# A MoE pair loop: the scatter chunks as one block behind the up product, and the gate multiply ahead of the adds

## The chip, the cores and the metric

The kernel runs on one core of a Trainium2 chip, as one launch. The metric is the device time of that launch in microseconds; lower is better.

## What is computed

The program is one inference step of a small hybrid decoder: 256 prompt tokens and 32 sample tokens (288 in all), width 1024, two layers. Each layer has a token mixer (recurrence and window attention in the first, dilated attention in the second), a normalisation, and a mixture of 64 experts. Only the expert part bears on the change:

```python
gate = jnp.take_along_axis(scores, top_e, axis=1)
gate = gate / jnp.sum(gate, -1, keepdims=True) * ROUTED_SCALE
...
def expert_block(args):
    xb, e = args
    hb = jax.nn.silu(xb @ w_gate[e]) * (xb @ w_up[e])
    return hb @ w_down[e]
...
routed = jax.ops.segment_sum(y_sorted.astype(F32) * gate_sorted[:, None], tok_sorted, num_segments=N)
```

For each expert the tokens routed to it are picked out, put through a SwiGLU of width 256, multiplied by their gates, and added back to the rows of the tokens.

## The kernel before

Experts are taken two at a time. Such a pair is numbered n, and q = n % 2 says which half of the double buffers it uses. Each layer has 32 pairs. Every engine runs its own program, and semaphores alone tie them together; the order on an engine is the order in which the code is written. TensorE (PE) does, for pair n, in `step`:

- `gather_pe` (L1200): the tokens of the pair, 64 slots for each of the two experts, are picked out of the bf16 parts of the activations by a matrix of zeros and ones that GpSimd made. It comes in two halves of 28 matmuls.
- `hidden_pe` (L1236): two transposes of the hidden values of pair n-1. It waits for `s_h2`, which VectorE signals when it has multiplied by the gate.
- `turn_pe` (L1208, L1211): the pick matrix is turned for the way back.
- `down_pe` (L1247): the down product of pair n-1, in fp32.
- `up_pe` (L1225): the gate and up products of pair n, in fp32. Eight slices `c` of the width, two experts each; the outputs of the two experts lie in partitions 0 to 63 and 64 to 127 of the same bank. An fp32 matmul shows as two MATMUL records, so a slice `c` is four records, and the whole product 32. Behind the last slice PE signals `s_gu`.
- `scatter_pe` (L1260): the outputs of pair n-1 are spread back over the 288 token rows. Eight chunks of 128 features; each is three bf16 matmuls of 288 columns (three parts of the fp32 value) into bank 6 or 7, by turns.

ScalarE (ACT) takes the silu (L1345) when `s_gu` comes. VectorE (DVE) then multiplies silu, up product and the gate of the slot (L1388, `hidden`), and adds each scattered chunk to the accumulator in SBUF (L1395, `add`). DVE also forms the second and third bf16 part of the down product (L1377, L1382, `outputs`).

Two waits matter for the change. A scatter chunk writes the bank of the chunk two before it, so it waits until that one has been added:

```python
pe.wait_ge(s_add[L], NC * n + c + NC - 1)
```

and an add waits for its chunk (`s_scat`). The sync queue (SP) fetches the experts' weights. The gate and up weights of a pair two ahead are issued (L1772) when `s_gu` says that the slots have been read, the down weights (L1779) on `s_dn`, which `down_pe` signals.

`over_pairs` runs `first` for pair 0, `step` for pairs 1 to 31, and `last` for what is left of pair 31. In `last` the eight scatter chunks stand one behind another with nothing between them.

Of the kernel before, what the change touches and what calls it, by code (L numbers as in the profile page):

```python
# [27 lines left out]
NC = D // P  # L28
# [100 lines left out]
def build(nc, a, o):  # L129

    ctx = ExitStack()
    with ctx:
# [86 lines left out]
        def slot_of(m):  # L219
            return m % RING  # L220
# [972 lines left out]
        def gather_pe(pe, L, n, q, hf):  # L1193

            pe.wait_ge(s_pm[L], 7 * n + 13)
            for c in range(4 * hf, 4 * hf + 4):
                for k in range(7):
                    m = 3 * NSA if k == 6 else P
                    lhs = xb[0:m, k].rearrange("t (f c) -> t c f", c=NC)[:, c, :]
                    ins = pe.matmul(ps[:, hf, (c % 4) * P:(c % 4 + 1) * P], lhs, pm[0:m, q, k // 3, :],  # L1200
                                    start=k == 0, stop=k == 6)
            ins.then_inc(s_ga[L], 1)

        def turn_pe(pe, L, n, q):

            for t in range(3):
                m = ROWS[t]
                pe.transpose(ps[:, 3, :].bitcast(BF16)[:, t * P:t * P + m], pm[0:m, q, t, :], ident_b[0:m, 0:m])  # L1208
            for t in range(3):
                m = ROWS[t]  # L1210
                ins = pe.matmul(ps[:, 3, NT:NT + 1], MO["pg"][0:m, q, t, :], ones[0:m, 0:1], start=t == 0, stop=t == 2)  # L1211
            ins.then_inc(s_pgt[L], 1)

        def up_pe(pe, L, n, q, it, scatter=None):

            pe.wait_ge(s_xg[L], 2 * n + 2)
            for u in range(2):
                s = slot_of(EXP0[L] + 2 * q + u)  # L1220
                pe.wait_ge(s_ring[L][s], static_dma[L][s] + (it + 1) * 32)
            for c in range(NC):
                for u in range(2):
                    w = ring[:, slot_of(EXP0[L] + 2 * q + u), 0:4096].rearrange("p (g c n) -> p c g n", g=2, c=NC)
                    ins = pe.matmul(ps[64 * u:64 * u + CAP, 2, :], MO["xg"][:, c, u * CAP:(u + 1) * CAP], w[:, c],  # L1225
                                    start=c == 0, stop=c == NC - 1)
                if c == NC - 1:
                    ins.then_inc(s_gu[L], 1)
                for chunk in {4: (0, 1), 5: (2, 3), 6: (4, 5), 7: (6, 7)}.get(c, ()) if scatter else ():
                    scatter(chunk)  # L1230

        def hidden_pe(pe, L, n):

            pe.wait_ge(s_h2[L], n + 1)
            for j in range(2):
                ins = pe.transpose(ps[:, 2, j * P:(j + 1) * P], MO["h"][:, j * P:(j + 1) * P], ident)  # L1236
            ins.then_inc(s_ht[L], 1)

        def down_pe(pe, L, n, q, it):

            pe.wait_ge(s_htc[L], n + 1)
            pe.wait_ge(s_ring_dn[L][q], (it + 1) * 32)
            for hf in range(2):
                for j in range(2):
                    for u in range(2):
                        w = ring[:, slot_of(EXP0[L] + 2 * q + u), 4096:6144].rearrange("p (j n) -> p j n", j=2)
                        ins = pe.matmul(ps[64 * u:64 * u + CAP, 4 + hf, :], MO["hT"][:, j, 64 * u:64 * u + CAP],  # L1247
                                        w[:, j, hf * BANK:(hf + 1) * BANK], start=j == 0, stop=j == 1)
            ins.then_inc(s_dn[L], 1)

        def scatter_pe(pe, L, n, q, c):

            if c == 0:
                pe.wait_ge(s_yc[L], 4 * n + 4)
                pe.wait_ge(s_pgtc[L], n + 1)

            pe.wait_ge(s_add[L], NC * n + c + NC - 1)
            for k in range(3):
                lhs = yb[:, k].rearrange("p (f c) -> p c f", c=NC)[:, c, :]
                ins = pe.matmul(ps[:, 6 + c % 2, 0:NT], lhs, pgt[:, q, :], start=k == 0, stop=k == 2)  # L1260
            ins.then_inc(s_scat[L], 1)

        def over_pairs(eng, L, first, step, last):

            more = iterations(eng)
            first(0, 0, 0)
            with eng.Fori(0, more) as i:
                step(2 * i + 1, 1, i)
                step(2 * i + 2, 0, i + 1)
            step(2 * more + 1, 1, more)  # L1270
            last(2 * more + 1, 1, more)
            return more

        def moe_pairs_pe(pe, L):
            pe.wait_ge(s_acc0, 8 * L + NC)
            pe.wait_ge(s_disp, L + 1)
            pe.wait_ge(s_xb, 10 * (L + 1))

            def first(n, q, it):
                gather_pe(pe, L, n, q, 0)  # L1280
                gather_pe(pe, L, n, q, 1)
                turn_pe(pe, L, n, q)
                up_pe(pe, L, n, q, it)

            def step(n, q, it):
                gather_pe(pe, L, n, q, 0)
                hidden_pe(pe, L, n - 1)
                gather_pe(pe, L, n, q, 1)
                turn_pe(pe, L, n, q)

                down_pe(pe, L, n - 1, 1 - q, it if q else it - 1)
                up_pe(pe, L, n, q, it, lambda c: scatter_pe(pe, L, n - 1, 1 - q, c))

            def last(n, q, it):
                hidden_pe(pe, L, n)
                down_pe(pe, L, n, q, it)
                for c in range(NC):
                    scatter_pe(pe, L, n, q, c)

            more = over_pairs(pe, L, first, step, last)  # L1300

            pe.wait_ge(s_add[L], more * (2 * NC) + 3 * NC)
            for t in range(3):
                m = ROWS[t]
                for c in range(NC):
                    ins = pe.transpose(ps[0:m, 2 * t + c // 4, (c % 4) * P:(c % 4 + 1) * P],
                                       MO["acc"][:, c, t * P:t * P + m], ident)
                ins.then_inc(s_f, 1)
# [58 lines left out]
        def moe_pairs_dve(v, L):  # L1367
            v.wait_ge(s_disp, L + 1)
            v.wait_ge(s_acc0, 8 * L + NC)
            v.sem_inc(s_add[L], NC)  # L1370

            def outputs(n):

                for hf in range(2):
                    half = slice(hf * BANK, (hf + 1) * BANK)
                    v.wait_ge(s_yb[L], 4 * n + hf + 1)
                    v.tensor_tensor(MO["y_rest"][:, half], ps[:, 4 + hf, :], yb[:, 0, half],  # L1377
                                    ALU.subtract).then_inc(s_yc[L], 1)
                for hf in range(2):
                    half = slice(hf * BANK, (hf + 1) * BANK)  # L1380
                    v.wait_ge(s_yb[L], 4 * n + hf + 3)
                    v.tensor_tensor(yb[:, 2, half], MO["y_rest"][:, half], yb[:, 1, half],  # L1382
                                    ALU.subtract).then_inc(s_yc[L], 1)

            def hidden(n, q):

                v.wait_ge(s_si[L], n + 1)
                v.scalar_tensor_tensor(out=MO["h"], in0=MO["sg"], scalar=MO["own_gate"][:, q:q + 1],  # L1388
                                       in1=ps[:, 2, DE:2 * DE], op0=ALU.mult, op1=ALU.mult).then_inc(s_h2[L], 1)

            def add(n, chunks=range(NC)):
                for c in chunks:
                    v.wait_ge(s_scat[L], NC * n + c + 1)
                    v.wait_ge(s_add[L], NC * n + c + 1)
                    v.tensor_tensor(MO["acc"][:, c, :], MO["acc"][:, c, :], ps[:, 6 + c % 2, 0:NT],  # L1395
                                    ALU.add).then_inc(s_add[L], 1)

            def first(n, q, it):
                hidden(n, q)

            def step(n, q, it):
                outputs(n - 1)
                add(n - 1, range(NC - 2))
                hidden(n, q)
                add(n - 1, range(NC - 2, NC))

            def last(n, q, it):
                outputs(n)
                add(n)

            more = over_pairs(v, L, first, step, last)
            v.wait_ge(s_add[L], more * (2 * NC) + 3 * NC)

# [717 lines left out]
```

## Time and profile before

| | |
|---|---|
| time, median of 3 runs | 1954.39 us (1952.23 to 1955.93) |
| span of the profiled execution | 1949.9 us |
| PE busy | 1825.8 us, 94% |
| DVE busy | 634.4 us, 33% |
| ACT busy | 471.5 us, 24% |
| GpSimd busy | 531.6 us, 27% |
| HBM | 305 GB/s over the span |

The profile gives the span from the first to the last instruction; of the profiled execution no other time is shown, and the median of the runs is 4.5 us above its span. PE stands for matmuls and PEld for the loading of their stationary operand, which goes on beside them.

### The profile page before, as it was taken

What the parts mean: (1) busy time and instruction counts of PE and PEld (TensorE: products, weight loads), DVE (VectorE), ACT (ScalarE), POOL (GpSimd) and SP (SyncE); (2) the same over time, 40 slices, a digit from 0 to 9 for tenths busy, and PEclk for the clock granted to TensorE, in tenths of its full rate; (3) what the DMA queues carried; (4) which work ended last, traced back from release to release, by engine and by line L of the source; (5) the groups of instructions that cost most, each with busy time, mean ns of one, the idle gap of its engine ahead of it and who ended that gap; (6) DMA issues with size and microseconds to landing.
All of it is one profiled execution on the core that took longest, in us unless ns stands there. A gap on an engine that the chain in (4) does not pass through costs nothing. (4 is left out here: it accounts for less than half of the span.)

```text
span 1949.9 us, 31977 instructions
## 1 busy us (share of the span) xinstructions
PE 1825.8 (94%) x11784; PEld 1119.5 (57%) x11784; DVE 634.4 (33%) x1444; ACT 471.5 (24%) x968; POOL 531.6 (27%) x1045
## 2 busy tenths in 40 slices
PE   7789999999999999978998978799999999999994
PEld 5563755555555555546777865375555555555552
DVE  4431523333232323342002343332323333333325
ACT  1431422222222222221002222322222222222222
POOL 1000453434333343201200000154343434243411
PEclk9859799999999999998997579889999999999997
DMA  9997188878888787845695355628787878787860
GB/s 309 334 321 255 65 324 319 345 310 337 320 325 331 316 343 309 347 160 218 212 331 205 129 184 184 274 89 333 314 343 308 345 312 347 310 343 314 341 263 25
DMA packets 113860, 540.81 MB, mean 277 GB/s; under 512 B 18821, under 2 KB 22661, under 8 KB 79636
## 3 DMA queue, kind: packets, MB, share of 16 engines
q1 hardware_dynamic: 110864, 481.67, 63.3%
q0 software_dynamic: 2880, 58.41, 8.8%
q8 instruction: 32, 0.52, 0.1%
q14 instruction: 16, 0.13, 0.0%
q10 hardware_dynamic: 68, 0.08, 0.0%
HBM read 535.69 MB, written 59.58 MB: 305 GB/s over the span
## 5 line engine op out<-in xcount | busy, mean ns | idle before, releaser
L1225 PE MATMUL ps<-ring,arena 128*64 128x512 f32 x2048 | 491.4, 601 | 0.0
L1260 PEld LDWEIGHTS ps<-arena 128*128 128x128 bf16 x1536 | 179.4, 148 | 214.0 <-DVE arena L1395 154.4
L1395 DVE TENSOR_TENSOR arena<-arena,ps 128x288 f32<-128x288 f32 x512 | 210.3, 451 | 228.7 <-PE ps L1260 228.5
L1188 POOL TENSOR_SCALAR arena<-arena 128x64 f32<-128x64 f32 x384 | 265.5, 710 | 0.0
L1225 PEld LDWEIGHTS ps<-ring,arena 128*64 128x64 f32 x2048 | 130.3, 136 | 220.6 <-issue 220.6
L1260 PE MATMUL ps<-arena 128*128 128x288 bf16 x1536 | 248.0, 298 | 7.3 <-DVE arena L1382 7.0
L1377 DVE TENSOR_TENSOR arena<-ps,arena 128x512 f32<-128x512 f32 x128 | 82.4, 686 | 520.0 <-ACT arena L1337 520.0
L1200 PE MATMUL ps<-arena 128*128 128x128 bf16 (+1 forms) x3584 | 245.4, 227 | 4.1 <-POOL arena L1188 4.1
L1200 PEld LDWEIGHTS ps<-arena 128*128 128x128 bf16 (+1 forms) x3584 | 241.7, 148 | 6.4 <-POOL arena L1188 4.8
L1247 PE MATMUL ps<-ring,arena 128*64 128x512 f32 x1024 | 233.8, 598 | 0.9 <-ACT arena L1325 0.9
L1176 POOL COPY arena<-misc 128x64 f32 x64 | 15.3, 238 | 703.0 <-POOLq L1173 703.0
L1186 POOL TENSOR_SCALAR arena<-arena 128x64 bf16<-128x64 f32 x384 | 159.6, 439 | 14.4 <-POOLq L1180 14.4
L1479 PE MATMUL ps<-xT,ring 128*128 128x288 f32 x576 | 143.1, 410 | 1.3 <-PE ps L1479 0.9
L1345 ACT ACTIVATE arena<-ps 128x256 f32<-128x256 f32 x64 | 24.8, 387 | 472.7 <-PE ps L1225 472.7
L1247 PEld LDWEIGHTS ps<-ring,arena 128*64 128x64 f32 x1024 | 67.8, 136 | 112.0 <-issue 109.6
L322 POOL TENSOR_TENSOR x_tok<-x_tok,gb 128x512 f32<-128x512 f32 (+1 forms) x12 | 20.9, 1739 | 404.8 <-DVE x_tok L360 404.8
L1479 PEld LDWEIGHTS ps<-xT,ring 128*128 128x128 f32 x576 | 109.8, 192 | 32.6 <-issue 2.7
L1337 ACT ACTIVATE arena<-ps 128x512 bf16<-128x512 f32 x128 | 69.5, 594 | 201.1 <-PE ps L1247 201.1
L1382 DVE TENSOR_TENSOR arena<-arena 128x512 bf16<-128x512 f32 x128 | 85.3, 706 | 6.4
L1341 ACT ACTIVATE arena<-arena 128x512 bf16<-128x512 f32 x128 | 78.6, 631 | 17.2 <-DVE arena L1377 17.2
L1315 ACT ACTIVATE arena<-ps 128x512 f32<-128x512 f32 x64 | 38.3, 599 | 144.4 <-PE ps L1200 144.4
L1388 DVE SCALAR_TENSOR_TENSOR arena<-arena,ps 128x256 f32<-128x256 f32 x64 | 30.8, 481 | 104.4 <-ACT arena L1345 104.4
(277 smaller groups left out, 1586.3 us busy)
## 6 DMA issues: line engine op xcount, KB each, us to landing
ring<-in_w_exp_gate SPq DMA_DIRECT2D x128, 1024.0 KB, 7.9
ring<-in_w_exp_up SPq DMA_DIRECT2D x128, 1024.0 KB, 9.9
ring<-in_w_exp_down SPq DMA_DIRECT2D x128, 1024.0 KB, 7.8
out_dil_kv_sample<-in_cache_dil_kv POOLq DMA_DIRECT2D x8, 4080.0 KB, 61.3
ring<-in_w_in_odd SPq DMA_DIRECT2D x6, 3072.0 KB, 15.1
out_dil_kv_sample<-in_cache_dil_kv POOLq DMA_DIRECT2D x8, 2032.0 KB, 38.6
ring<-in_cache_dil_kv SPq DMA_DIRECT2D x4, 2048.0 KB, 18.5
ring<-in_cache_dil_kv SPq DMA_DIRECT2D x32, 256.0 KB, 7.6
```

The lines of the kernel that those rows point to most:

```text
L1186: ins = pool.tensor_scalar(out, slots, pos[:, t, u:u + 1], None, ALU.is_equal)
L1188: ins = pool.tensor_scalar(out, slots, pos[:, t, u:u + 1], gate[:, t, u:u + 1], ALU.is_equal, ALU.mult)
L1200: ins = pe.matmul(ps[:, hf, (c % 4) * P:(c % 4 + 1) * P], lhs, pm[0:m, q, k // 3, :], start=k == 0, stop=k == 6)
L1225: ins = pe.matmul(ps[64 * u:64 * u + CAP, 2, :], MO["xg"][:, c, u * CAP:(u + 1) * CAP], w[:, c], start=c == 0, stop=c == NC - 1)
L1247: ins = pe.matmul(ps[64 * u:64 * u + CAP, 4 + hf, :], MO["hT"][:, j, 64 * u:64 * u + CAP], w[:, j, hf * BANK:(hf + 1) * BANK], start=j == ...
L1260: ins = pe.matmul(ps[:, 6 + c % 2, 0:NT], lhs, pgt[:, q, :], start=k == 0, stop=k == 2)
L1337: act.activation(yb[:, 0, hf * BANK:(hf + 1) * BANK], ps[:, 4 + hf, :], ACT.Copy).then_inc(s_yb[L], 1)
L1341: act.activation(yb[:, 1, half], MO["y_rest"][:, half], ACT.Copy).then_inc(s_yb[L], 1)
L1377: v.tensor_tensor(MO["y_rest"][:, half], ps[:, 4 + hf, :], yb[:, 0, half], ALU.subtract).then_inc(s_yc[L], 1)
L1382: v.tensor_tensor(yb[:, 2, half], MO["y_rest"][:, half], yb[:, 1, half], ALU.subtract).then_inc(s_yc[L], 1)
L1395: v.tensor_tensor(MO["acc"][:, c, :], MO["acc"][:, c, :], ps[:, 6 + c % 2, 0:NT], ALU.add).then_inc(s_add[L], 1)
L1479: ins = pe.matmul(ps[:, 2 + k % 4, 0:NT], w[:, c, (k % 6) * P:(k % 6 + 1) * P], xT[:, c, 0:NT], start=c == 0, stop=c == NC - 1)
```

## The change

On PE, `up_pe` loses the scatter chunks that stood behind its slices 4, 5, 6 and 7 (two behind each), and all eight chunks follow the whole up product. On DVE, `hidden`, which stood behind the sixth add, stands ahead of the first. No instruction is added or removed, and no semaphore changes its count.

```diff
-        def up_pe(pe, L, n, q, it, scatter=None):
+        def up_pe(pe, L, n, q, it):
...
                 if c == NC - 1:
                     ins.then_inc(s_gu[L], 1)
-                for chunk in {4: (0, 1), 5: (2, 3), 6: (4, 5), 7: (6, 7)}.get(c, ()) if scatter else ():
-                    scatter(chunk)
...
                 down_pe(pe, L, n - 1, 1 - q, it if q else it - 1)
-                up_pe(pe, L, n, q, it, lambda c: scatter_pe(pe, L, n - 1, 1 - q, c))
+                up_pe(pe, L, n, q, it)
+                for c in range(NC):
+                    scatter_pe(pe, L, n - 1, 1 - q, c)
...
             def step(n, q, it):
                 outputs(n - 1)
-                add(n - 1, range(NC - 2))
                 hidden(n, q)
-                add(n - 1, range(NC - 2, NC))
+                add(n - 1)
```

On PE, in `step`, this is the order before from the up product on (L1225 the up product, L1260 a scatter chunk, L1257 the setting of the value its wait compares with); the piece between slice 5 and slice 7 repeats:

```order
L1225 MATMUL ps<-ring,arena 64x512 x10
L1254 ISA
L1257 ISA
L1260 MATMUL ps<-arena 128x288 x3
L1257 REGISTER_ALU
L1260 MATMUL ps<-arena 128x288 x3
L1225 MATMUL ps<-ring,arena 64x512 x2
L1257 REGISTER_ALU
L1260 MATMUL ps<-arena 128x288 x3
```

And this is the same place in the change, where the scatter is L1258 and its wait value L1255:

```order
L1225 MATMUL ps<-ring,arena 64x512 x16
L1252 ISA
L1255 ISA
L1258 MATMUL ps<-arena 128x288 x3
L1255 REGISTER_ALU
L1258 MATMUL ps<-arena 128x288 x3
L1255 REGISTER_ALU
L1258 MATMUL ps<-arena 128x288 x3
```

The six up matmuls that stood in pairs behind the second, fourth and sixth chunk have moved ahead of the first. Behind the eighth chunk the gather of the next pair (L1200) follows, as before.

On DVE, in `step`, this is what stands around the multiply by the gate (L1388) before; L1395 is an add, and the rows end with the outputs of the next pair:

```order
L1395 TENSOR_TENSOR arena<-arena,ps 128x288
L1387 REGISTER_ALU
L1388 SCALAR_TENSOR_TENSOR arena<-arena,ps 128x256
L1393 REGISTER_ALU
L1395 TENSOR_TENSOR arena<-arena,ps 128x288
L1393 REGISTER_ALU
L1395 TENSOR_TENSOR arena<-arena,ps 128x288
L1376 ISA
```

In the change it stands behind the outputs (L1382) and ahead of the first add:

```order
L1382 TENSOR_TENSOR arena<-arena 128x512
L1387 REGISTER_ALU
L1388 SCALAR_TENSOR_TENSOR arena<-arena,ps 128x256
L1393 ISA
L1395 TENSOR_TENSOR arena<-arena,ps 128x288
L1393 REGISTER_ALU
L1395 TENSOR_TENSOR arena<-arena,ps 128x288
```

Six adds that stood ahead of the gate multiply now stand behind it.

## Rows read from the trace of the kernel before

**Rows 1.** The page: span and busy time of each engine.

```profile
span 1949.9 us, 31977 instructions
PE 1825.8 (94%) x11784; PEld 1119.5 (57%) x11784; DVE 634.4 (33%) x1444; ACT 471.5 (24%) x968; POOL 531.6 (27%) x1045
```

**Rows 2.** Waits, whole span: who for whom, us in total, times, longest.

```profile
PEld ps L1225 <- issue: 220.6, 834, 0.3
SPq L1772 <- PE ps L1225: 541.1, 60, 12.9
```

**Rows 3.** Matmuls of the timeline, 713 to 722 us: start, length, instruction, count.

```profile
713.92 0.96 PE L1260 MATMUL ps<-arena 128*128 128x288 bf16 x6
...
715.83 0.95 PE L1260 MATMUL ps<-arena 128*128 128x288 bf16 x6
...
719.62 0.96 PE L1260 MATMUL ps<-arena 128*128 128x288 bf16 x6
720.41 1.90 PE L1200 MATMUL ps<-arena 128*128 128x128 bf16 x28
```

**Rows 4.** ACT and DVE of the same timeline, one pair earlier for the first row.

```profile
700.49 0.39 ACT L1345 ACTIVATE arena<-ps 128x256 f32<-128x256 f32 x1 [7.42 <-PE ps L1225]
...
711.76 1.29 DVE L1382 TENSOR_TENSOR arena<-arena 128x512 bf16<-128x512 f32 x2
...
719.73 0.39 ACT L1345 ACTIVATE arena<-ps 128x256 f32<-128x256 f32 x1 [7.41 <-PE ps L1225]
720.16 0.48 DVE L1388 SCALAR_TENSOR_TENSOR arena<-arena,ps 128x256 f32<-128x256 f32 x1 [0.99 <-ACT arena L1345]
720.55 0.81 DVE L1395 TENSOR_TENSOR arena<-arena,ps 128x288 f32<-128x288 f32 x2
```

**Rows 5.** Chain that ended last: the up product where no scatter stands in it.

```profile
1902.47 4.29 PE ps L1225 x20
```

**Rows 6.** The gate multiply's line: how many, first and last.

```profile
L1388 DVE SCALAR_TENSOR_TENSOR arena<-arena,ps x64: 480/481/483, 259.3 to 1912.9; 128x256 f32<-128x256 f32 x64
```

**Rows 7.** Timeline behind the last pair, where eight chunks stand alone.

```profile
1913.47 0.20 PEld L1236 LDWEIGHTS ps<-square,arena 128*128 128x128 f32 x2 [0.37 <-DVE arena L1388]
...
1921.52 0.70 PEld L1260 LDWEIGHTS ps<-arena 128*128 128x128 bf16 x6 [4.36 <-issue]
1922.15 0.82 DVE L1395 TENSOR_TENSOR arena<-arena,ps 128x288 f32<-128x288 f32 x2 [0.76 <-PE ps L1260]
1922.66 0.77 PEld L1260 LDWEIGHTS ps<-arena 128*128 128x128 bf16 x6 [0.44 <-DVE arena L1395]
...
1923.29 0.45 DVE L1395 TENSOR_TENSOR arena<-arena,ps 128x288 f32<-128x288 f32 x1 [0.32 <-PE ps L1260]
1923.80 0.43 PEld L1260 LDWEIGHTS ps<-arena 128*128 128x128 bf16 x3 [0.38 <-DVE arena L1395]
...
1924.78 0.45 DVE L1395 TENSOR_TENSOR arena<-arena,ps 128x288 f32<-128x288 f32 x1 [0.35 <-PE ps L1260]
...
1926.27 1.06 DVE L1395 TENSOR_TENSOR arena<-arena,ps 128x288 f32<-128x288 f32 x2 [0.31 <-PE ps L1260]
```

**Rows 8.** The same place in narrower windows: the second add and the fourth chunk apart.

```profile
1922.52 0.45 DVE L1395 TENSOR_TENSOR arena<-arena,ps 128x288 f32<-128x288 f32 x1
1923.02 0.40 PEld L1260 LDWEIGHTS ps<-arena 128*128 128x128 bf16 x3
```

**Rows 9.** Busy time by stretch: length, PE, PEld, DVE, ACT, POOL, granted clock, DMA share, GB/s.

```profile
700.00:860.00 160.00, 159.30 (x1140) 87.46 (x1136) 51.47 (x107) 37.98 (x83) 43.06 (x90) 1.00 0.69 275
1310.00:1900.00 590.00, 590.00 (x4275) 327.88 (x4275) 189.68 (x391) 142.08 (x308) 216.17 (x451) 1.00 0.81 323
1913.00:1918.00 5.00, 4.41 (x21) 1.35 (x19) 1.14 (x3) 0.38 (x1) 0.00 (x0) 1.00 0.00 0
1918.00:1921.50 3.50, 0.04 (x2) 0.00 (x0) 2.58 (x4) 2.31 (x4) 0.00 (x0) 1.00 0.00 0
1921.50:1927.40 5.90, 5.15 (x25) 2.94 (x25) 3.54 (x8) 0.00 (x0) 0.00 (x0) 0.71 0.00 1
```

## Prediction

> **What bounds the kernel now.** The page first: PE is busy for 94% of the span, every other engine for about a third or less [rows 1]. Then the stretches: in both pair loops PE is busy for practically all of the time (159.3 of 160 us in the first layer, 590 of 590 in the second) at a granted clock of 1.00, 2.4 GHz [rows 9]. So in the loops the time is the length of PE's own queue, and whatever holds PE lengthens the pair. From silu to silu a pair takes 719.73 - 700.49 = 19.24 us [rows 4]. There are 64 gate multiplies, 32 pairs in each of two layers [rows 6]; `step` runs for 31 of them in a layer, so whatever the change does in `step` counts 62 times.
>
> The weights don't bound it. The loads of gate and up weights wait 541.1 us for PE to have read the slots, and the idle time of PE's weight loading in the up product is "issue" and no transfer [rows 2]; the DMA share in the loops is 0.69 and 0.81 [rows 9]. In the change `s_gu` comes some 3 us earlier within the pair, so the loads are issued earlier: that queue gains cover and loses none.
>
> **The scatter before.** Chunk 0 starts at 713.92, chunk 6 at 719.62, and the gather of the next pair at 720.41 [rows 3]. Of the 5.70 us from chunk 0 to chunk 6, three slices of the up product would take 3 x 0.858 = 2.57 by themselves (20 records in 4.29 us, four to a slice [rows 5]). Six woven chunks therefore cost 3.13 us, and the last two 0.79: 3.92 us of PE for eight chunks. The adds cost PE nothing here: chunks 0 and 1 are added while slice 5 runs.
>
> **What the same chunks cost as one block.** The kernel already has such a block, behind the last pair [rows 7]. It shows what the weave hides. I count from the first weight load of chunk 0.
> - A chunk's first weight load to the start of its add: 1922.15 - 1921.52 = 0.63 us; again 1923.29 - 1922.66 = 0.63.
> - Start of that add to the first weight load of the chunk that reuses the bank: 1922.66 - 1922.15 = 0.51; again 1923.80 - 1923.29 = 0.51.
> - So one round trip of a bank is 1.14 us. Two banks alternate, so a chunk can follow every 0.57 us, where PE alone needs 0.79 / 6 x 3 = 0.40 [rows 3]. The block is paced by the trip between PE and DVE, not by PE.
> - The second add starts 0.37 behind the first, and the fourth chunk's weights 0.50 behind that [rows 8]: bank 7 runs the same trip, about 0.37 behind bank 6.
>
> Ahead of the first add now stands the gate multiply. In the old order it starts 720.16 - 719.62 = 0.54 after the first weight load behind the up product, and an add follows it at 720.55, 0.93 after [rows 3, 4]. In the change that load is chunk 0's, so add 0 starts at 0.93 where its data are there at 0.63: the gate costs 0.30 us once per pair. Now along both banks:
> - add 0 at 0.93, add 1 at 1.30;
> - weights of chunk 2 at 0.93 + 0.51 = 1.44, of chunk 3 at 1.80;
> - chunks 4 and 6 at 2.58 and 3.72; chunks 5 and 7 at 2.94 and 4.08;
> - chunk 7 takes PE 0.40 more, so the gather of the next pair starts at 4.48.
>
> Before, the gather came 0.79 after the same point. The tail grows by 3.69 us, and 3.13 us of weaving ahead of it fall away: **+0.56 us a pair**.
>
> **What else moves.** Everything in PE's queue behind the block is later by the same 0.56: gathers, transposes, down product. The hidden transposes don't wait: the gate is done by about 1.0 us, and they stand behind the block and half a gather. The second and third output parts end 711.76 + 1.29 = 713.05, 0.87 before chunk 0 started; chunk 0 now starts 2.57 later still, so that wait has more cover. Adds 6 and 7 end by about 5.1, beside the gather, and the next adds are some 15 us away. Behind the last pair of each layer the transposes waited 0.37 us for the gate [rows 7]; that goes, twice, -0.7 us. Edits costed at nothing are thus covered by a gather of 1.9 us or more.
>
> **Sum.** 62 x 0.56 = 34.7, less 0.7: +34 us. The rows come from an execution with a span of 1949.9 us; the median of the runs is 4.5 above it, and I take that distance to stay. 1954.4 + 34 = **1988 us**.
>
> The unknown terms: if the gate multiply cost no delay, the block would be 0.30 shorter, -19 us, 1970. If a round trip took 1.49 us, as from 1924.78 to 1926.27 further on in the same block (two chunks there [rows 7]), three of them would add 1.05 us a pair, +65, 2053. But the granted clock fell in that stretch, to a mean of 0.71 [rows 9], which the loop hasn't shown; the first rows of the block, before it fell, are the nearer ones. A round trip that is 0.1 us off moves the time by 19 us.
>
> **Rivals.**
> *PE isn't held, and the block wins.* Changing between 64-column and 128-column work costs: a round of two chunks and a slice takes 715.83 - 713.92 = 1.91, against 0.79 + 0.86 = 1.65, so 0.26 a round, and three rounds go away. If the adds kept up, 24 matmuls at 0.13 would take 3.16 instead of 3.92: -0.76 a pair, -47 us, **1907 us**. It decides at the round trip: the three on the path give back the 0.56 if each takes 0.95 instead of 1.14, and everything if it is at or under 0.79. Against it stand the waits on L1395 in the block of the last pair [rows 7], with the trip measured at 1.14. Chance 7%. The Trainium skill (TensorEngine Tiling (Array Packing), section Key Properties) says that changing the tiling mode drains the engine; taken alone it speaks for the block, since six of the eight changes in this stretch of a pair go. The 0.26 us of a round agrees with it.
>
> *The clock falls.* The block gives PE gaps that the loop doesn't have: about 0.5 us without a matmul behind chunk 1, 0.2 to 0.4 between later chunks. Behind the last pair the clock fell (mean 0.71 in 5.9 us, so about 3.4 us at the lower level, 1.2 GHz) after PE had stood for 3.5 us [rows 9]. Over the 5 us before that, with stops of 0.59 us in all, it had stayed at 1.00 [rows 9]. If each pair brought one such stretch, it would cost between 0.9 us (five chunks at about 0.75 instead of 0.57) and 1.7 us (dense work at half rate): +56 to +105 on top, about **2070 us**; if one pair in four did, 2008. No gap of the block comes near 3.5 us. Chance 6% for enough of it to leave the range. The Trainium skill (TensorE: Matmul & The Clock Gate, section "A second HAM failure mode: psum-queue depth-cycling") reports a kernel whose short stops between groups on alternating banks made the clock swing. No row of this trace shows that in a loop.
>
> *It comes out even.* The round trip is shorter than in the last block, since here DVE's later adds have their wait values ready, and lands near 0.95: within 4 us of **1954**. Chance 3%.
>
> *A longer trip without the clock,* because the gather's ACT work and the weight writes share the memories with the adds: the adds in the loop take the same 0.81 for two as in the tail, with DMA running, which speaks against it. 2020 to 2050; chance 5%.
>
> **How the numbers follow.** The forecast has 79%, with a range of its own of 1972 to 2008: the gate's bound below, 0.1 us more a trip above. The range for everything is the same but for a little on top: **1972 to 2010**. A measurement of this kernel can tell about 0.2%, 4 us, from no change. Slower by more than that: forecast, clock and longer trip, 79 + 6 + 5 = 90%; same 3%; faster 7%.
>
> **What the profile of the change would show.** The pair period at 19.8 us. The up product as 32 records in a row. Waits of PE's weight loads for the adds in every block, four or more starts apart by 0.57 on average, the first gap (after chunk 1) about 0.7 us of weight loading. The gate multiply 0.54 after chunk 0's first weights, the gather 4.5 after. The clock at 1.00 throughout the loops. I am wrong if chunks follow each other at 0.40, if the clock row shows fives in the loops, or if a wait for the ring appears ahead of the up product.

## The result and the profile after

The changed kernel takes 1991.42 us (median of 4 runs, 1990.54 to 1991.88), the kernel before 1953.41 (1952.23 to 1955.93). The ratio is 1.0194, with a 95% interval of 1.018 to 1.0209: slower by 38 us, where 34 were forecast and 1988 us predicted. The interval lies clear of no change.

The page of the changed kernel, its first lines, the clock in 40 slices (tenths of full speed, 9 is 90% or more), and two groups of the list of costly instructions (busy, mean ns | idle before, and what ended it); last a stretch of the second loop (length, busy time of PE, PEld, DVE, ACT, POOL, granted clock, DMA share, GB/s):

```profile
span 1989.2 us, 31977 instructions
...
PE 1813.0 (91%) x11784; PEld 1128.3 (57%) x11784; DVE 635.2 (32%) x1444; ACT 471.5 (24%) x968; POOL 531.7 (27%) x1045
...
PEclk9859799999999999998997579799999999999998
...
L1258 PE MATMUL ps<-arena 128*128 128x288 bf16 x1536 | 248.5, 298 | 59.1 <-DVE arena L1395 52.1
L1258 PEld LDWEIGHTS ps<-arena 128*128 128x128 bf16 x1536 | 173.1, 148 | 170.0 <-DVE arena L1395 103.4
...
1320.00:1900.00 580.00, 554.62 (x4073) 318.04 (x4074) 177.37 (x365) 135.17 (x293) 219.96 (x463) 1.00 0.82 318
```

The instructions are the same in number. PE's share has gone from 94% [rows 1] to 91%, and the matmuls of the scatter (now L1258) now stand idle for DVE's adds, 52.1 us in all. The clock is at its full level in the loops: 1.00 in the stretch of the second one, where PE is now busy for 554.62 of 580 us, and nines in the slices of the first.

One pair in the timeline of the changed kernel (start, length, engine, instruction; in brackets the idle time before and what ended it); it answers to [rows 3] and [rows 4]:

```profile
751.83 0.70 PEld L1258 LDWEIGHTS ps<-arena 128*128 128x128 bf16 x6 [0.81 <-issue]
...
751.95 0.39 ACT L1345 ACTIVATE arena<-ps 128x256 f32<-128x256 f32 x1 [4.28 <-PE ps L1225]
752.37 0.48 DVE L1388 SCALAR_TENSOR_TENSOR arena<-arena,ps 128x256 f32<-128x256 f32 x1 [3.91 <-ACT arena L1345]
752.77 0.81 DVE L1395 TENSOR_TENSOR arena<-arena,ps 128x288 f32<-128x288 f32 x2
753.27 0.70 PEld L1258 LDWEIGHTS ps<-arena 128*128 128x128 bf16 x6 [0.74 <-DVE arena L1395]
...
753.90 0.83 DVE L1395 TENSOR_TENSOR arena<-arena,ps 128x288 f32<-128x288 f32 x2 [0.32 <-PE ps L1258]
754.41 0.70 PEld L1258 LDWEIGHTS ps<-arena 128*128 128x128 bf16 x6 [0.44 <-DVE arena L1395]
...
755.55 0.70 PEld L1258 LDWEIGHTS ps<-arena 128*128 128x128 bf16 x6 [0.43 <-DVE arena L1395]
...
756.35 1.89 PE L1200 MATMUL ps<-arena 128*128 128x128 bf16 x28
```

The reader should go down the weight loads of L1258. They come in groups of six, two chunks each, at 751.83, 753.27, 754.41 and 755.55: 1.44, 1.14 and 1.14 us apart, where two chunks in a row take PE 0.79 [rows 3]. Each of the last three groups was released by an add. The first gap is longer because the gate multiply (L1388) stands ahead of the first add; the first experiment shows that. The gather follows at 756.35, 4.52 after the first load.

The silu rows of four successive pairs of the changed kernel, which answer to the two of [rows 4]:

```profile
732.02 0.39 ACT L1345 ACTIVATE arena<-ps 128x256 f32<-128x256 f32 x1 [4.28 <-PE ps L1225]
751.95 0.39 ACT L1345 ACTIVATE arena<-ps 128x256 f32<-128x256 f32 x1 [4.28 <-PE ps L1225]
771.76 0.39 ACT L1345 ACTIVATE arena<-ps 128x256 f32<-128x256 f32 x1 [4.28 <-PE ps L1225]
791.68 0.39 ACT L1345 ACTIVATE arena<-ps 128x256 f32<-128x256 f32 x1 [4.28 <-PE ps L1225]
```

A pair takes about 19.92 or 19.81 us by turns, 19.87 on average, against 19.24 before. 62 x 0.63 = 39 us, and the span has grown by 1989.2 - 1949.9 = 39.3.

### The profile page after: what moved, and what is told of

It is laid out like the page before. It is cut to its first block and busy times, and to the rows that moved or that the text cites. A ratio compares the mean times of both kernels' runs of the same rounds, so it can differ in the third digit from the quotient of the medians.

```text
span 1989.2 us, 31977 instructions
## 1 busy us (share of the span) xinstructions
PE 1813.0 (91%) x11784; PEld 1128.3 (57%) x11784; DVE 635.2 (32%) x1444; ACT 471.5 (24%) x968; POOL 531.7 (27%) x1045
## 5 line engine op out<-in xcount | busy, mean ns | idle before, releaser
L1225 PE MATMUL ps<-ring,arena 128*64 128x512 f32 x2048 | 450.4, 592 | 0.0
L1225 PEld LDWEIGHTS ps<-ring,arena 128*64 128x64 f32 x2048 | 146.9, 137 | 291.2 <-issue 291.2
L1258 PE MATMUL ps<-arena 128*128 128x288 bf16 x1536 | 248.5, 298 | 59.1 <-DVE arena L1395 52.1
L1258 PEld LDWEIGHTS ps<-arena 128*128 128x128 bf16 x1536 | 173.1, 148 | 170.0 <-DVE arena L1395 103.4
L1200 PE MATMUL ps<-arena 128*128 128x128 bf16 (+1 forms) x3584 | 246.4, 227 | 4.1 <-POOL arena L1188 4.1
L1200 PEld LDWEIGHTS ps<-arena 128*128 128x128 bf16 (+1 forms) x3584 | 239.6, 147 | 10.6 <-POOL arena L1188 4.8
L1245 PE MATMUL ps<-ring,arena 128*64 128x512 f32 x1024 | 233.8, 598 | 0.9 <-ACT arena L1325 0.9
L1395 DVE TENSOR_TENSOR arena<-arena,ps 128x288 f32<-128x288 f32 x512 | 210.9, 452 | 63.7 <-PE ps L1258 63.0
L1245 PEld LDWEIGHTS ps<-ring,arena 128*64 128x64 f32 x1024 | 67.8, 136 | 112.0 <-issue 109.6
L1388 DVE SCALAR_TENSOR_TENSOR arena<-arena,ps 128x256 f32<-128x256 f32 x64 | 30.8, 482 | 287.2 <-ACT arena L1345 287.2
L1382 DVE TENSOR_TENSOR arena<-arena 128x512 bf16<-128x512 f32 x128 | 85.3, 706 | 6.4
```

## The experiments

Three theories went into the first of them. **A:** each scatter bank makes a round trip between PE and DVE of 1.14 us, which paces a block on two banks, and the gate multiply adds 0.30 once. **B:** the gate multiply alone holds the block. **C:** the block costs PE more whatever DVE does. The converse of the first experiment, the gate multiply ahead of the adds with the chunks still woven into two banks, would never end. The gate needs the whole up product; the last slices of the up product would stand behind chunk 2; chunk 2 waits for add 0; and add 0 would stand behind the gate. Each of them would wait for the next.

**The gate multiply back in its place** (changed kernel, block kept):

```diff
                 outputs(n - 1)
+                add(n - 1, range(NC - 2))
                 hidden(n, q)
-                add(n - 1)
+                add(n - 1, range(NC - 2, NC))
```

> Changed kernel with the gate multiply back behind the sixth add; the chunks stay one block. Theory A (the block is paced by the 1.14 us round trip of each of two banks, and the gate multiply adds 0.30 us once): add 0 starts 0.63 after chunk 0's weights instead of 0.93, everything behind it 0.30 earlier, 62 x 0.30 = 19 us less: 1973. Theory B (the gate multiply, which has to wait for the silu, is what holds the adds and so the block; without it the block costs what the weave did): 1953. Theory C (the chunks cost PE more as a block whatever DVE does): 1991.

Measured: 1973.94 us (1972.19 to 1975.94), ratio to the kernel before 1.0105 [1.0088, 1.0122]. That is A to within 1 us: of the 38 us lost, 17 are the gate's place (1991.4 - 1973.9) and 21 the block's. Its timeline of matmuls shows the stops evened out:

```profile
746.30 0.96 PE L1258 MATMUL ps<-arena 128*128 128x288 bf16 x6
747.44 0.96 PE L1258 MATMUL ps<-arena 128*128 128x288 bf16 x6 [0.18 <-DVE arena L1395]
748.58 0.96 PE L1258 MATMUL ps<-arena 128*128 128x288 bf16 x6 [0.18 <-DVE arena L1395]
749.72 0.96 PE L1258 MATMUL ps<-arena 128*128 128x288 bf16 x6 [0.18 <-DVE arena L1395]
750.52 1.89 PE L1200 MATMUL ps<-arena 128*128 128x128 bf16 x28
```

1.14 us three times, and the gather 4.22 after the first chunk, where it was 4.51 in the changed kernel (4.52 from the first weight load). B, which gave 1953, is out as the whole cause, and C, which gave 1991, as well.

**One bank instead of two:**

```diff
-            pe.wait_ge(s_add[L], NC * n + c + NC - 1)
+            pe.wait_ge(s_add[L], NC * n + c + NC)
...
-                ins = pe.matmul(ps[:, 6 + c % 2, 0:NT], lhs, ...
+                ins = pe.matmul(ps[:, 6, 0:NT], lhs, ...
```

(and the same bank in the add).

> Changed kernel with all scatter chunks in bank 6, each waiting for the add before it: the suspected round trip counts seven times instead of three. Theory A: chunk 1 at 0.93 + 0.51 = 1.44, then one every 1.14, chunk 7 at 8.28, the gather at 8.7 instead of 4.5: +4.2 us a pair, 2252; more if the clock falls, since PE then works for a third of 8 us. Theory B: the gate counts once, as now, and the bank matters little: 1991 to 2010. Theory C: 1991.

Measured: 2464.69 us (two runs, 2464.12 and 2465.27), ratio 1.2621 [1.2596, 1.2646]. Both B and C had it at 1991 to 2010 at most, so both are out. But it is 213 us above the 2252 of the trips alone. The timeline of matmuls, and the stretches of the same pair (length, PE, PEld, DVE, ACT, POOL, granted clock, DMA share, GB/s), show why:

```profile
738.42 0.59 PE L1258 MATMUL ps<-arena 128*128 128x288 bf16 x3
739.85 0.59 PE L1258 MATMUL ps<-arena 128*128 128x288 bf16 x3 [0.84 <-DVE arena L1395]
740.99 0.59 PE L1258 MATMUL ps<-arena 128*128 128x288 bf16 x3 [0.55 <-DVE arena L1395]
742.13 0.59 PE L1258 MATMUL ps<-arena 128*128 128x288 bf16 x3 [0.55 <-DVE arena L1395]
743.27 0.94 PE L1258 MATMUL ps<-arena 128*128 128x288 bf16 x3 [0.55 <-DVE arena L1395]
744.76 0.94 PE L1258 MATMUL ps<-arena 128*128 128x288 bf16 x3 [0.55 <-DVE arena L1395]
746.25 0.94 PE L1258 MATMUL ps<-arena 128*128 128x288 bf16 x3 [0.55 <-DVE arena L1395]
747.74 0.94 PE L1258 MATMUL ps<-arena 128*128 128x288 bf16 x3 [0.55 <-DVE arena L1395]
748.48 3.19 PE L1200 MATMUL ps<-arena 128*128 128x128 bf16 x28
```

```profile
738.40:743.20 4.80, 2.38 (x14) 1.32 (x12) 2.20 (x5) 0.39 (x1) 0.00 (x0) 0.96 0.70 267
743.20:752.00 8.80, 7.08 (x43) 5.14 (x44) 1.83 (x5) 0.29 (x1) 0.00 (x0) 0.50 0.79 332
752.00:765.00 13.00, 13.00 (x84) 6.50 (x84) 2.58 (x4) 3.97 (x9) 7.41 (x15) 0.96 0.39 139
```

The first five chunks follow at 1.43 and then 1.14 three times, as A has it. Then the clock is at 0.50 for the 8.8 us of the middle stretch: a chunk takes 0.94 instead of 0.59, the trip 1.49 instead of 1.14, and the first gather half 3.19 instead of 1.89. It comes back while PE is busy without a stop. The same 8.8 us at 0.50 stand in the three pairs that follow, 27.3 us apart, and the mean clock is 0.81 from 700 to 1000 us and from 1600 to 2200, so this goes on pair after pair. Three trips at 1.49 (1.05 us), the last chunk (0.74 to the gather, 0.34 more) and the first gather half (1.30) are 2.7 us a pair; the 213 us are 3.4 a pair, and the second gather half, slower too, stands between the two.

**Four banks, block and gate as in the change:**

```diff
-            pe.wait_ge(s_add[L], NC * n + c + NC - 1)
+            pe.wait_ge(s_add[L], NC * n + c + NC - 3)
...
-                ins = pe.matmul(ps[:, 6 + c % 2, 0:NT], lhs, ...
+                ins = pe.matmul(ps[:, (6, 7, 4, 5)[c % 4], 0:NT], lhs, ...
...
             pe.wait_ge(s_htc[L], n + 1)
+            pe.wait_ge(s_add[L], NC * n + NC)
```

(the same banks in the add; the last line is in `down_pe`, whose banks 4 and 5 are).

> Changed kernel with the scatter in four banks, 6, 7, 4, 5 by turns (4 and 5 are the down product's, free by then; the down product waits for all adds of the pair before). The gate multiply stays ahead of the adds. Theory A: chunk 4 needs add 0, done for it at 1.44, where PE comes to it at 1.6: no wait is left, the block takes 24 matmuls at 0.13 = 3.2 us instead of 4.5, the turns into and out of 64-column work stay saved: 1.3 x 62 = 81 us less than the change, about 1910, faster than the kernel before. Theory B: the gate still holds the adds, at most 19 us less: 1972. Theory C: 1991.

Measured: 1894.03 us (1892.92 to 1895.16), ratio 0.9701 [0.9685, 0.9717]. Theory A had 1910, 16 us more. So the waits were all of the loss, and without them the block is faster than the weave. Two successive pairs of it, and DVE in the first:

```profile
732.60 3.17 PE L1259 MATMUL ps<-arena 128*128 128x288 bf16 x24
735.61 1.94 PE L1200 MATMUL ps<-arena 128*128 128x128 bf16 x28
...
750.95 3.17 PE L1259 MATMUL ps<-arena 128*128 128x288 bf16 x24
753.96 1.89 PE L1200 MATMUL ps<-arena 128*128 128x128 bf16 x28
...
733.13 0.48 DVE L1389 SCALAR_TENSOR_TENSOR arena<-arena,ps 128x256 f32<-128x256 f32 x1 [3.98 <-ACT arena L1346]
733.53 3.00 DVE L1396 TENSOR_TENSOR arena<-arena,ps 128x288 f32<-128x288 f32 x8
```

The 24 matmuls run without a stop and take 3.01 us to the gather, though the first add still starts behind the gate multiply, 0.93 after the first chunk. The pair takes 750.95 - 732.60 = 18.35 us. I had put the block at 3.2: 0.19 x 62 = 12 of the 16 us.

**Four banks, woven:** the kernel before with the same edit.

> Kernel before (woven, gate behind the sixth add) with the same four banks. Theory A: the weave had already hidden the round trip, so more banks give nothing: 1953, within 4 us. If four banks help for a reason of their own (another bank for PE's writes than the one DVE reads, for instance), this kernel gains too, and the gain of the four-bank block would not be the round trip's.

Measured: 1951.66 us (1949.34 to 1953.67, 10 runs), ratio 0.9993 [0.9983, 1.0003]. More banks give the weave nothing, so the gain above isn't one of other banks as such.

**Three banks,** 6, 7 and 4 by turns, in the changed kernel; a chunk then waits for the add three before it.

> The changed kernel with three scatter banks, 6, 7, 4 by turns. Theory A (each bank makes a round trip of 1.14 us, PE needs 0.37 a chunk): chunk 3 needs add 0, so 1.44, where PE would come at 1.14, and from there three chunks take 1.10 and the trip 1.14, so the two nearly match; chunk 7 at 2.95, the gather at 3.37, against 4.52 with two banks and 3.01 with four. 0.36 x 62 = 22 us more than four banks: 1916. If the gain of four banks came from something else than the trip, three would lie halfway, about 1943, or not gain at all.

Measured: 1919.15 us (1917.92 to 1920.05), ratio 0.983 [0.9814, 0.9846]. 3 us above A, and not halfway. One row has the block and one the gather:

```profile
743.79 3.54 PE L1259 MATMUL ps<-arena 128*128 128x288 bf16 x24
747.22 1.95 PE L1200 MATMUL ps<-arena 128*128 128x128 bf16 x28
```

3.43 us, where 3.37 were worked out. The weight loads of the same block show one stop:

```profile
743.78 1.07 PEld L1259 LDWEIGHTS ps<-arena 128*128 128x128 bf16 x9 [0.81 <-issue]
745.22 1.84 PEld L1259 LDWEIGHTS ps<-arena 128*128 128x128 bf16 x15 [0.36 <-DVE arena L1396]
```

Chunk 3 comes 1.44 behind the first load, as worked out, where three chunks in a row take 3.01 / 8 x 3 = 1.13, and 0.31 of the 0.42 us that this block is longer than the four-bank one are that one wait behind the delayed first add. The pace of a trip over three banks (0.38 a chunk) lies too close to PE's own to be told from it here.

**Four banks, the gate multiply back behind the sixth add:**

> Four banks, one block, and the gate multiply back behind the sixth add. Theory A: with four banks nothing waits for the adds, so the 0.30 us that the gate multiply delays them is covered: the same as four banks with the gate ahead, 1894 within 4 us. Theory B (the gate multiply ahead of the adds has a cost of its own, wherever it stands in the trip): 19 us less, 1875.

Measured: 1895.42 us (1892.07 to 1898.0), ratio 0.9715 [0.9699, 0.9731], the same as with the gate ahead. The gate's place costs something only where PE waits for the adds.

**Four banks, one round of the weave kept:** chunks 0 and 1 ahead of the last slice, the rest as a block, gate ahead.

```diff
+                if scatter and c == NC - 2:
+                    scatter(0)
+                    scatter(1)
```

> Four banks, gate ahead, but chunks 0 and 1 stand ahead of the last slice of the up product: one more turn from 64-column to 128-column work and back, and no wait for an add (these two chunks need only the adds of the pair before). Theory D (each round of such turns costs PE about 0.29 us, a third of the 0.88 us by which a pair of the four-bank block is shorter than one of the kernel before): 62 x 0.29 = 18 us more, 1912. Rival: the turns are free and the woven kernel lost its 0.88 us elsewhere, for instance in waits for the adds: 1894.

Measured: 1958.57 us (1957.91 to 1959.7), ratio 1.0037 [1.0024, 1.0049]: 64 us above the plain four-bank block, not 18. The expectation had missed a wait. Its timeline:

```profile
737.86 0.96 PE L1262 MATMUL ps<-arena 128*128 128x288 bf16 x6
738.75 1.08 PE L1225 MATMUL ps<-ring,arena 128*64 128x512 f32 x4
739.76 0.96 PE L1262 MATMUL ps<-arena 128*128 128x288 bf16 x6
741.21 1.70 PE L1262 MATMUL ps<-arena 128*128 128x288 bf16 x12 [0.48 <-DVE arena L1399]
...
740.30 0.48 DVE L1392 SCALAR_TENSOR_TENSOR arena<-arena,ps 128x256 f32<-128x256 f32 x1 [5.02 <-ACT arena L1349]
740.70 3.00 DVE L1399 TENSOR_TENSOR arena<-arena,ps 128x288 f32<-128x288 f32 x8
```

Chunks 0 and 1 are ready by 739, but their adds stand behind the gate multiply at 740.30, which needs the whole up product. Chunk 4 therefore waits for add 0 until 741.21, where chunks 2 and 3 alone would have let it go at about 740.51 (two chunks of the unbroken block take 3.01 / 4 = 0.75). That is 0.70 us a pair, 43 of the 64 us.

**The same with the gate multiply behind the sixth add:**

> The previous kernel (four banks, chunks 0 and 1 ahead of the last up slice) with the gate multiply back behind the sixth add. In the previous one the adds of chunks 0 and 1 stood behind the gate multiply, which waits for the whole up product, so chunk 4 waited for add 0; here they can run during slice 7 and nothing waits. So only the extra round of turns between 64- and 128-column work is left. Theory D: 0.29 us a pair over the plain four-bank block, 62 x 0.29 = 18, 1912. If the turns are free: 1894. If the previous kernel's loss had nothing to do with the gate: 1958.

Measured: 1914.0 us (1910.78 to 1916.14), ratio 0.9805 [0.9787, 0.9822]. With that wait gone, one round of turns costs (1914.0 - 1895.4) / 62 = 0.30 us a pair. The runs of either kernel spread over 5 to 6 us, 0.1 a pair, but the timeline says the same:

```profile
739.26 0.96 PE L1262 MATMUL ps<-arena 128*128 128x288 bf16 x6
740.14 1.08 PE L1225 MATMUL ps<-ring,arena 128*64 128x512 f32 x4
741.16 2.43 PE L1262 MATMUL ps<-arena 128*128 128x288 bf16 x18
743.42 1.89 PE L1200 MATMUL ps<-arena 128*128 128x128 bf16 x28
```

From chunk 0 to chunk 2 it is 1.90 us, and 1.90 - 0.86 (the slice) - 0.75 (two chunks) = 0.29.

## Why the prediction was right

*What bounds the kernel:* right. In all experiments the time followed from what stands in PE's queue for a pair and what holds it there, times 62; in the one-bank run the clock came on top.

*The round trip* (0.63 + 0.51 = 1.14, read from the two chunk pairs behind the last pair) was the step that carried the forecast, and it held in the loop to 0.01 us with one bank (at full clock) and with two; three banks gave the time worked out from it to 3 us. Chunks 2, 4 and 6 were put at 1.44, 2.58 and 3.72 us behind the first weight load, and came at 1.44, 2.58 and 3.72.

*The gate's delay* of 0.30 us: right. The two-bank block measured 4.22 without it and 4.51 with it, from chunk 0 to the gather, and the time differs by 17 us where 19 were worked out.

*The gather's start* was put at 4.48 and came at 4.52. I had put chunk 7 0.36 us behind chunk 6, at the distance of the adds, and given it 0.40. In the rows it is 0.80 from chunk 6 to the gather, which is what two chunks take PE anyway (0.79 [rows 3]).

*The sum* was 34 us; the medians are 38 apart and the two profiled spans 39.3. Held against the spans, 0.04 x 62 = 2.5 us are the gather's start, and every second pair of the changed kernel takes 0.11 us more, 31 x 0.11 = 3.4. With these the sum is 39.9. The 0.11 is not the chunks, which follow at the same distances in both kinds of pair. About half of it comes before the gather (4.57 us from chunk 0 to the gather in one, 4.51 in the other) and half in the gather's first row (1.95 against 1.89). Its cause stays open. It needs no wait for an add, since the four-bank block shows 1.94 and 1.89 without one. PE's loop turns behind every second block, but that alone doesn't do it: with four banks and the gate multiply in its old place the same rows are 1.89 and 1.90, and in the kernel before 1.91 and 1.90. The 0.7 us saved behind the last pairs is there: nothing waits for the gate multiply any more.

*The rival that the block wins:* its mechanism is real and its condition wasn't met. I had put the break-even at a trip of 0.95 and the full gain at 0.79 or less. With four banks a trip of 1.14 covers four chunks instead of two, and the full gain is there: 59 us less than the kernel before, where I had worked out 47 from 0.76 a pair. The measured term is 19.24 - 18.35 = 0.89 a pair, 55 us; the other 4 lie outside the pairs and weren't followed up. The 0.76 was too small because it took 0.13 for each of 24 matmuls, 3.16 us, and the unbroken block takes 3.01. For the same reason one round of turns is 0.29 to 0.30 us, not the 0.26 that I read off. The Trainium skill's rule that changing the tiling mode drains the engine (TensorEngine Tiling (Array Packing), section Key Properties) agrees with these runs, which give a round its price. They don't show that the tiling mode is the reason: the work changes from fp32 to bf16 at the same places, and no run took the two apart. The rule was right about the direction of that one term; with two banks the waits outweighed it.

*The rival of the clock* did not come about with two banks, where the stops are 0.48 and 0.18 us, and did with one bank. So the 6% stood for a thing that exists nearby, and the reason given against it, that no stop came near 3.5 us, was not a good one; the last section says why.

*Weights:* right; no wait for the weights of the experts appeared, not even at 18.35 us a pair.

## What to carry to other kernels

A stretch in which a producer and a consumer alternate over few banks has a floor of its own: the round trip divided by the number of banks. Here one bank and two ran at that floor. Read the trip where the trace already shows it bare, here behind the last pair, and compare it with the producer's own time for a chunk. If the floor is higher, weave other work in or add banks. Here adding banks was better (1894 us against 1953), because each round of the weave cost 0.3 us; other work woven in may cost less or more. And an instruction moved ahead in a queue holds everything behind it until its own operand is there: name that operand before moving it.

## What the runs showed of the hardware

- PE's clock fell in a loop in which PE never stood long: 0.84 us at most in the pair shown, and no wait for an add over 0.9 in the whole run. With one bank PE was busy for 2.38 of 4.80 us, at a clock of 0.96, and the 8.8 us that followed ran at 0.50 (1.2 GHz), in each of the four pairs looked at. With two banks, PE busy for 3.67 of 4.50 us of the block and stops of 0.48 and 0.18 us, it stayed at 1.00. I had argued that no stop came near the 3.5 us that preceded the fall in [rows 9]; that was the wrong comparison, since many short stops did the same. The Trainium skill reports such a swing for a kernel that cycles through PSUM banks (TensorE: Matmul & The Clock Gate, section "A second HAM failure mode: psum-queue depth-cycling"). This run agrees as far as short stops between groups of matmuls made the clock swing; it used one bank and did not cycle.
- One round of turns between the 64-column fp32 products and the 128-column bf16 scatter (into the scatter and back) cost 0.30 us by the times and 0.29 by the timeline, though PE's rows in the profile show no idle time there.
- The trip from a chunk's first weight load through DVE's add back to the next weight load on that bank is 1.14 us at full clock and 1.49 at half, with one bank. The longer matmuls of the chunk account for the difference: 0.94 - 0.59 = 0.35.
